# An encoder layer's first stage on one core: the bias row's place, and the order of the next quarter's norm

## The reference, cut to what matters

```
h = rms_norm(x, g_mix)                 # x * rsqrt(mean(x*x) + eps) * g
proj = h @ w_in                        # here: q (512 columns), k (128), v (128)
q = rms_norm(q by heads of 64, q_gain); k = rms_norm(k by heads, k_gain)
bias = rel_bias[t5_bucket(key - query)]   # -inf where |key - query| > 128
```

## Time and profile before

| | us |
|---|---|
| median of 3 runs | 3527.59 |
| lowest, highest | 3523.97, 3529.44 |
| the profiled execution | 3525.42 |
| its span on the core | 3523.6 |
| PE busy | 3072.8 (87%) |
| DVE, ACT, POOL busy | 1546.6, 1071.4, 785.8 |

### The profile page before, as it was taken

One profiled execution on the slowest core, in us unless ns is written; L12 is line 12 of the kernel. 1 busy time (PEld: TensorE's weight loads), 2 busy tenths in 40 slices (PEclk: granted clock), 3 DMA queues, 4 the chain that ended last, 5 costly groups with the idle time before them and its releaser, 6 DMA issues. The chain is left out here.

```text
span 3523.6 us, 64121 instructions
## 1 busy us (share of the span) xinstructions
PE 3072.8 (87%) x26764; PEld 2465.0 (70%) x26764; DVE 1546.6 (44%) x1959; ACT 1071.4 (30%) x2041; POOL 785.8 (22%) x937
## 2 busy tenths in 40 slices
PE   5777998998472799999699779999999999799999
PEld 2545556886242789899466558888888888688887
DVE  2555552333355455453344374444444444333333
ACT  2333552111342344444324231111111111222222
POOL 2343551000235667663123150000000000000000
PEclk7888999999785999999899989999999999899999
DMA  4222112331346333321465231111111111522331
GB/s 109 90 87 64 37 37 50 73 74 48 122 180 225 100 108 108 108 79 40 153 198 181 90 122 39 52 50 52 48 48 48 48 48 42 225 89 56 95 96 36
DMA packets 214174, 313.19 MB, mean 89 GB/s; under 512 B 63257, under 2 KB 138393, under 8 KB 210874
## 3 DMA queue, kind: packets, MB, share of 16 engines
q1 hardware_dynamic: 212506, 308.74, 27.7%
q10 hardware_dynamic: 1440, 1.18, 0.1%
HBM read 208.16 MB, written 101.71 MB: 88 GB/s over the span
## 5 line engine op out<-in xcount | busy, mean ns | idle before, releaser
L91 PE MATMUL up_p<-h_hi,up_w_hi 128*128 128x512 f32 x1408 | 550.4, 391 | 40.5 <-DVE h_lo L1956 37.5
L92 PE MATMUL up_p<-h_lo,up_w_hi 128*128 128x512 f32 x1408 | 549.6, 390 | 0.0
L93 PE MATMUL up_p<-h_hi,up_w_lo 128*128 128x512 f32 x1408 | 549.3, 390 | 0.0
L91 PEld LDWEIGHTS up_p<-h_hi,up_w_hi 128*128 128x128 f32 x1408 | 265.2, 188 | 97.9 <-issue 42.9
L1908 ACT COPY up_raw<-up_p 128x512 f32<-128x512 f32 x176 | 103.2, 588 | 749.7 <-PE up_p L93 749.6
L93 PEld LDWEIGHTS up_p<-h_hi,up_w_lo 128*128 128x128 f32 x1408 | 265.4, 189 | 55.5
L92 PEld LDWEIGHTS up_p<-h_lo,up_w_hi 128*128 128x128 f32 x1408 | 265.6, 189 | 55.2
L91 PE MATMUL down_p<-down_act_hi,down_w_hi 128*128 128x512 f32 x704 | 275.0, 391 | 22.9 <-DVE down_act_lo L2113 22.9
L1966 DVE TENSOR_SCALAR up_con<-up_raw,vecs_sb 128x2048 f32<-128x2048 f32 x44 | 59.3, 1347 | 515.8 <-ACT up_raw L1908 515.8
L92 PE MATMUL down_p<-down_act_lo,down_w_hi 128*128 128x512 f32 x704 | 274.8, 390 | 0.0
L93 PE MATMUL down_p<-down_act_hi,down_w_lo 128*128 128x512 f32 x704 | 274.6, 390 | 0.0
(11 more groups left out here) (232 smaller groups left out, 6294.5 us busy)
## 6 DMA issues: line engine op xcount, KB each, us to landing
rec_inp<-gate_chunks SPq DMA_DIRECT2D x64, 512.0 KB, 3.5
up_w<-in_w_up SPq DMA_DIRECT2D x44, 512.0 KB, 4.0
act_out<-up_con SPq DMA_DIRECT2D x22, 1024.0 KB, 4.3
down_act<-act_out SPq DMA_DIRECT2D x88, 256.0 KB, 3.2
gate_chunks<-gates_out SPq DMA_DIRECT2D x4, 4096.0 KB, 11.8
first_w<-in_w_attn SPq DMA_DIRECT2D x24, 512.0 KB, 3.7
rkv_chunks<-rwkv_project_mix SPq DMA_DIRECT2D x12, 1024.0 KB, 6.4
down_w<-in_w_down SPq DMA_DIRECT2D x22, 512.0 KB, 13.3
```

The source lines that it names most:

```text
L91: pe.matmul(out, w_hi, x_hi, start=start, stop=False)
L92: pe.matmul(out, w_hi, x_lo, start=False, stop=False)
L93: return pe.matmul(out, w_lo, x_hi, start=False, stop=stop)
```

## The change

Four edits, all in `first_block`:
- `onehot`, `outside` and `row` lie in `v_tok` instead of in `raw` and `head_sq`. The waits in `take` for the bias go; `copy_v` of the first quarter waits for the bias write instead.
- ACT: `root(n + 1)` runs in item m = 2, behind `take`, instead of in item m = 3 between `head_root` and `take`.
- DVE: in items m = 3, 4, 5 the next quarter's work (`invert`; `low`) stands ahead of `normed` instead of behind it.
- POOL: the eight `scale` operations are spread 2, 3, 3 over m = 3, 4, 5 instead of 4, 4 over m = 3, 4. `high` and `low` stay 4, 4 over m = 4, 5.

```
+    SCALE = {3: range(0, 2), 4: range(2, 5), 5: range(5, 8)}
+    HIGH = {4: range(0, 4), 5: range(4, 8)}
...
-        onehot, outside, row = raw[0:32, 0], raw[0:1, 1], head_sq[0:AH, 0]
+        early = K.v_tok.rearrange("p b t -> p (b t)")
+        onehot, outside, row = early[0:32, 0:512], early[0:1, 512:1024], early[0:AH, 1024:1536]
...
                 def copy_v(g):
                     n = g // MT
+                    if n == 0:
+                        done(act, "bias_out", 16)
                     done(act, "turned", n + 1)
...
                 def take(g):
                     done(act, "projected", g + 1)
-                    if g == 0:
-                        done(act, "bias_row", 1)
-                    if g == 0 or g == 1:
-                        done(act, "bias_out", 16)
...
                         if m in (1, 2):
                             squares(n + 1, range(4 * (m - 1), 4 * m))
-                        elif m == 3:
-                            root(n + 1)
                         elif m >= 4:
-                            high(n + 1, range(4 * (m - 4), 4 * (m - 3)))
+                            high(n + 1, HIGH[m])
                     take(g)
+                    if n + 1 < TN and m == 2:
+                        root(n + 1)
...
                     if g + 1 < ITEMS:
                         split(g + 1)
-                    if n + 1 < TN and m in (3, 4):
-                        scale(n + 1, range(4 * (m - 3), 4 * (m - 2)))
+                    if n + 1 < TN and m >= 3:
+                        scale(n + 1, SCALE[m])
...
                 def body(g, n, m):
+                    if n + 1 < TN and m == 3:
+                        invert(n + 1)
+                    if n + 1 < TN and m >= 4:
+                        low(n + 1, HIGH[m])
                     if g >= 1 and is_qk(g - 1):
                         normed(g - 1)
-                    if n + 1 < TN:
-                        if m == 3:
-                            invert(n + 1)
-                        elif m >= 4:
-                            low(n + 1, range(4 * (m - 4), 4 * (m - 3)))
```

## The result

The changed kernel takes 3481.68 us (median of 4 runs, 3480.37 to 3484.66); the kernel before, measured beside it, 3525.78 us. The ratio is 0.9873, interval 0.9858 to 0.9889: about 44 us faster. The profiled execution's span is 3480.0 us, 43.6 less. The forecast was 3483.

What follows compares the result with a forecast made beforehand. First stage bound by TensorE's waits behind item 1 and at three changes of quarter; 3 x 14.6 + 1.1 = 44.9 us off 3527.6 gives 3483 us, range 3475 to 3502.

Steps and rivals of the forecast that it cites:

- Part 1: Bias row's wait in the first quarter: weight block 2 still lands at 67.9, so the squares come only 1.1 us earlier.
- The list of part 2: Engine steps at each of three changes of quarter: item 13 starts 15.4 us early, 14.6 us with the clock.
- The clock: PE's granted clock may dip in the thin stretch at each change of quarter: up to 2.5 us, taken as 0.8.
- Rival A: Change of quarter: low 3 starts after split(12) on the shared ports, delaying block 13; gain 31 us, 3496; chance 0.21.
- Rival B: Bias wait is a real 22 us: block 2 lands without the write, Part 1 gains about 21; 3462, chance 0.07.
- Rivals C and D: Clock stays 0.50 after item 12: C loses 10.5 us a quarter, 3558; D eats the gain, 3527; chance 0.04 each.

Runs made afterwards that it cites:

- e1: Kernel before with only the bias row, one-hot and mask row moved to the values' tile and the bias waits to copy_v; 3527.8 us, ratio 0.9994.
- e3: Changed kernel with the 2 MB bias write cut into eight 256 KB pieces, one issued in each of items 1 to 8; 3458.5 us, again 3456.8.
- e0: The changed kernel run again unaltered, with a second trace; 3480.5 us, ratio 0.9855 to the kernel before.
- e5: Changed kernel with the scales back at 4 and 4 in items m = 3 and 4; 3499.8 us, ratio 0.9912.
- e9: e3 with only the scales changed, to 3, 3 and 2; 3461.1 us, ratio 0.9796.
- e10: e5 with high and low split 3 and 5 instead of 4 and 4, so low 3 comes later; 3488.1 us, ratio 0.9875.
- e4: Changed kernel with VectorE's order put back, normed ahead of invert and low; 3521.5 us, ratio 0.9973.
- e8: e3 with scales 3, 3, 2, q's store one item later behind the next block's load, and block 7 cast before take(5); 3451.2 us, ratio 0.9775.

## Why the prediction was right

- Part 1. The mechanism is shown twice, by e1 (the wait removed: nothing) and by e3 (the transfer moved: 24.9 us). I had 1.1 us for it. In the first trace the second squares stand at 83.82 instead of 85.35, which with the 0.44 of later loads is 2.0 us. Half is the head root's earlier start, as forecast, and half is that the squares, begun 0.7 us sooner, took 5.53 us instead of 6.39, as more of them ran at full clock (the clock of 71 to 76 us reads 0.70, before 0.50). That half is chance: in e1 they took 6.55 and the gain was 1.0.
- The list of part 2 held step for step. Set against the squares of their quarter (mine at 154.25, the trace's at 137.00, so 17.25 apart), I had split(11) end at 169.6, the trace has 152.32, or 169.57; normed(8) 170.1 and 170.1; lows 0 to 3 from 172.2 to 176.2, the trace 172.2 to 176.1; split(12) ending 178.4 and 178.3; store of q 180.4 and 180.2; item 13 at 187.95, the trace 188.05. The stretch was 33.7 by the list and is 33.8. PE's idle pieces were 1.2, 0.8, 1.0 and 1.4 by the list and are 1.22, 0.49, 0.73 and 1.65.
- The clock was the term that was off: I took 0.8 us a quarter for a dip, and the changed kernel has none. The three changes give 15.7, 15.3 and 15.4 us, not 14.6, and the first stage 47.9 us instead of 44.9. The later stages' chance took 4 back in the first measurement, so the total came closer there (44.1 in medians against 44.9) than its terms deserve; in e0's it is 48.4. That part of the total is luck.
- Rival A did not happen in the changed kernel: low 3 ended as split(6) began. That it was a real price at a margin of a few tenths is what e5 showed when the scales were crowded. The Trainium skill's rule (SBUF — State Buffer, "SBUF: two separate sides"), that the first to take the shared ports keeps them for the instruction, fits e5's 2.83 us beside a split of 2.79: the low began 0.51 behind it and ended 0.55 behind it. I had priced A at 10 to 13 us of gain left per quarter; e5 left 12.4 in the stretch (49.5 - 37.1), and with the clock 10.6 ((47.9 - 14.1 - 2.0) / 3).
- Rival B is refuted by e1. Rivals C and D, a clock that stays low through several items behind item 12, did not occur; a dip of about one item's length is the most that was seen there (e5, e9, e10).
- The three edits of part 2 are not worth their sum. Each put back alone costs 34 (DVE's order), 14.5 (root) and 14.1 us (scales) at attention's start, together more than the 47.9 that all give: each lies on the same chain.

## What to carry to other kernels

When a long wait is to be removed, ask what the same engine needs next and whether it stands behind the same cause: here the wait on a transfer hid the wait for a load queued behind that transfer, and only moving the transfer paid. Write the steps of every engine against the clock of one quarter, including the ports that two engines share; margins of a few tenths of a microsecond decide who is held 2.8. Waiting of TensorE costs its own length and then the clock: in e4 6.6 us more of it made the stretch 10.9 longer, and of the change's 15.7 us 4.8 are the clock given back.

## What the hardware showed that I had not expected

- How idle time lies before an item may decide its clock, but the length of the gap alone does not. e9 and e3 start item 7 at the same place (33.9), with PE's idle time in one piece of 2.75 us or in pieces of 0.73 and 1.74, and only the first met 0.53 in its windows; e9's three gaps of 2.40 to 2.75 were all followed by a lower clock, one of 2.05 in e3's first trace was not. In e8, pieces of 0.53 and 1.80 us stand before item 13, and the clock of 145 to 149 us reads 0.71; nearly the same pieces (0.49 and 1.80) before item 7 left it at 1.00.
- A write of 2 MB out of 8 partitions moved at about 50 GB/s and made the issue of a following 512 KB load take 14.39 us on SP; with nothing ahead the same issue took 0.33 us (e3). Whether the few partitions make it slow no run shows.
